# Expert stage of a two-layer diffusion transformer step: 25 tiles of 128 rows, or 14 tiles of four 32-row lists

## What is computed

```python
def moe(h, w_router, router_bias, w_gate_l, w_up_l, w_down_l):
    t = h.reshape(B * N, D)
    scores = jax.nn.sigmoid((t @ w_router).astype(F32))
    sel = scores + router_bias.astype(F32)
    grp = sel.reshape(-1, N_EXPERT_GROUPS, EXPERTS_PER_GROUP)
    best = jnp.argmax(lax.top_k(grp, TOP_K)[0].sum(-1), axis=-1)
    ...
    _, idx = lax.top_k(masked, TOP_K)          # best group, then two experts in it
    w = jnp.take_along_axis(scores, idx, axis=-1)
    w = w / jnp.sum(w, axis=-1, keepdims=True)
    combine = jnp.sum(jax.nn.one_hot(idx, N_EXPERTS, dtype=F32) * w[..., None], axis=1)
    gate = jnp.einsum('td,edf->tef', t, w_gate_l)
    up = jnp.einsum('td,edf->tef', t, w_up_l)
    act = jax.nn.silu(gate) * up * combine[..., None].astype(gate.dtype)
    return jnp.einsum('tef,efd->td', act, w_down_l).reshape(B, N, D)
```

## Time and profile before

| | us |
|---|---|
| median of three runs | 2057.49 |
| lowest and highest run | 2054.66, 2057.91 |
| profiled execution: span, first to last instruction | 2054.5 |
| TensorE busy | 1912.6 (93%) |
| VectorE busy | 1080.4 (53%) |
| ScalarE busy | 884.8 (43%) |
| POOL busy | 314.5 (15%) |
| mean granted TensorE clock | 0.976 of full |
| bytes moved | 336.34 MB, 164 GB/s over the span |

### The profile page before, as it was taken

The page is one execution under the profiler, slowest core; times in us unless marked ns, Lnnn a source line. Parts: engine busy times, 40 slices in busy tenths (PEclk is TensorE's granted clock), DMA queues, the critical chain, the costliest instruction groups (busy, mean ns, idle before and its releaser), DMA issues. The chain is left out here.

```text
span 2054.5 us, 31276 instructions
## 1 busy us (share of the span) xinstructions
PE 1912.6 (93%) x12731; PEld 1617.7 (79%) x12731; DVE 1080.4 (53%) x1766; ACT 884.8 (43%) x1423; POOL 314.5 (15%) x120
## 2 busy tenths in 40 slices
PE   6999999999999979999779998898999998899993
PEld 4899866699999857777578997677999987577762
DVE  4385367641433256777573734665243334577763
ACT  4443455532222235566454435555222233466653
POOL 1303100032224120000111121000212331000003
PEclk9999999999999999999979999999999999999996
DMA  7422477725612159999441220002222222999954
GB/s 262 131 62 64 147 247 256 240 88 199 211 62 73 47 212 361 315 309 318 156 167 44 75 72 13 1 1 92 89 67 72 73 68 114 376 422 369 311 189 174
DMA packets 163921, 336.34 MB, mean 164 GB/s; under 512 B 10434, under 2 KB 121666, under 8 KB 149316
## 3 DMA queue, kind: packets, MB, share of 16 engines
q1 hardware_dynamic: 151488, 299.63, 41.9%
q0 software_dynamic: 5760, 20.97, 2.7%
q10 hardware_dynamic: 6532, 13.74, 2.1%
HBM read 334.58 MB, written 53.74 MB: 189 GB/s over the span
## 5 line engine op out<-in xcount | busy, mean ns | idle before, releaser
L728 POOL TENSOR_TENSOR wlo<-raw,whi 128x2048 fp32r<-128x2048 f32 x46 | 216.1, 4697 | 1053.2 <-ACT whi L752 1053.2
L2007 DVE TENSOR_TENSOR xw_gu_lo<-xw_gu_raw,xw_gu_hi 128x2048 fp32r<-128x2048 f32 x96 | 218.9, 2284 | 53.7 <-ACT xw_gu_hi L1788 35.6
L171 PE MATMUL psum<-h_hi,whi 128*128 128x320 f32 (+2 forms) x896 | 215.3, 313 | 9.0 <-DVE h_lo L156 6.5
L171 PE MATMUL psum<-h_hi,wlo 128*128 128x320 f32 (+2 forms) x896 | 213.0, 310 | 0.0
L171 PE MATMUL psum<-h_lo,whi 128*128 128x320 f32 (+2 forms) x896 | 213.0, 310 | 0.0
L171 PE MATMUL psum<-whi,h_hi 128*128 128x256 f32 x720 | 210.2, 292 | 0.5 <-ACT v_tok L866 0.5
L171 PE MATMUL psum<-wlo,h_hi 128*128 128x256 f32 x720 | 203.6, 283 | 0.0
L171 PE MATMUL psum<-whi,h_lo 128*128 128x256 f32 x720 | 203.6, 283 | 0.0
L1788 ACT ACTIVATE xw_gu_hi<-xw_gu_raw 128x2048 fp32r<-128x2048 f32 x96 | 178.1, 1907 | 7.6 <-DMA xw_gu_raw<-w_e_up 7.6
L2159 PE MATMUL psum<-xw_d_raw,act_T 128*128 128x512 f32 x400 | 179.9, 592 | 0.9 <-ACT act_T L1818 0.9
L832 ACT ACTIVATE prob<-psum,small_stats 128x640 f32<-128x640 f32 (+1 forms) x160 | 112.0, 705 | 133.1 <-DVE small_stats L1194 133.0
(11 more groups left out here) (319 smaller groups left out, 3657.3 us busy)
## 6 DMA issues: line engine op xcount, KB each, us to landing
xw_d_raw<-w_e_down SPq DMA_DIRECT2D x50, 1024.0 KB, 9.0
xw_gu_raw<-w_e_gate SPq DMA_DIRECT2D x48, 1024.0 KB
xw_gu_raw<-w_e_up SPq DMA_DIRECT2D x48, 1024.0 KB
raw<-w_in SPq DMA_DIRECT2D x46, 1024.0 KB, 5.4
wm_rest<-w_mod SPq DMA_DIRECT2D x40, 1024.0 KB, 5.3
y_rows<-y_sel SPq DMA_DIRECT2D x50, 512.0 KB, 9.5
h_sel<-h_rows SPq DMA_DIRECT2D x48, 512.0 KB, 7.5
h_rows<-c_zero ACTq DMA_DIRECT2D x5, 2560.0 KB, 11.2
```

Source lines behind the costliest of these rows:

```text
L171: mm = pe.matmul(dst, st, mv[q], start=start and n == 0, stop=stop and n == 2)
L728: pool.tensor_tensor(wlo[i % 2][:, :, :], raw[i % 2][:, :, :], whi[i % 2][:, :, :].bitcast(F32), ALU.subtract).then_inc(w_lo, 1)
L2007: dve.tensor_tensor(gu_lo[i % 2][:, n, :, :], gu_raw[i % 2][:, n, :, :], gu_hi[i % 2][:, n, :, :].bitcast(F32), ALU.subtract).then_inc(x_l ...
```

## The change

The rows of all experts are laid out in places (slots) of 32 rows, each of one expert: 56 places, in four lists of 14. Tile s has place s of each list, 32 rows of four lists, so that a tile's four quarters can be of four experts. Each list has one copy of its expert's weights on the chip, plain fp32, in three parts: the first half of gate and up by input dimension, the second half, and down. A part is loaded anew only where the list's expert changes; the condition is in a table that VectorE makes. The host lays the weights out in this order (`expert_parts`). The products are whole fp32 products with 32 stationary columns, one after another for the four lists into the four quarters of a bank; nothing is rounded and subtracted. The first tile's rows are read from `h_rows` as the others' are. Loads of rows and most stores of results move from SyncE to ScalarE's queue, a store becomes four of 32 rows, the clearing of `h_rows` covers 14 and not 25 tiles.

```diff
-N_OVER = (2 * TOK - NE) // P
-N_TILES = NE + N_OVER
-SLOTS = N_TILES * P
+N_LISTS, SLOT = 4, 32
+N_SLOTS = (2 * TOK + (SLOT - 1) * NE) // SLOT
+N_TILES = -(-N_SLOTS // N_LISTS)
+N_SLOTS = N_TILES * N_LISTS
...
+        part_at = ((64, 72, 80), (16, 24, 32), (40, 48, 56), (88, 96, 104))
+        xw = [[at(f"xw{q}_{c}", [P, 2048], Z + off * K) for c, off in enumerate(offs)] for q, offs in enumerate(part_at)]
...
                 def _(sp):
+                    w_exp = a["w_expert"][layer].rearrange("e c p n -> c e p n")
...
+                    def list_load(s, q):
+                        v = sp.value_load(slot_i[0:1, q, s:s + 1], min_val=0, max_val=2 * NE - 1)
+                        return v % NE, v < NE
+                    def load_part(c, q, expert, cond):
+                        sp.dma_start(xw[q][c][:, :], w_exp[c][expert, :, :], cond=cond,
+                                     bounds_check="skip_entire_dma").then_inc(xw_ld[c], 16)
...
+                    sp.wait_ge(g_pfree, 24)
+                    for c in range(2):
+                        sp.dma_start(xw[0][c][:, :], w_exp[c][0]).then_inc(xw_ld[c], 16)
+                    sp.wait_ge(o_full, KD)
+                    sp.dma_start(routes[:, :], a["c_route"].partition_broadcast(P)).then_inc(r_c, 16)
+                    sp.dma_start(xw[0][2][:, :], w_exp[2][0]).then_inc(xw_ld[2], 16)
                     low_ready(sp, N_STREAM - 1)
+                    sp.wait_ge(r_st, TAB_STEPS)
+                    firsts = [sp.value_load(slot_i[0:1, q, 0:1], min_val=0, max_val=NE - 1) for q in range(1, N_LISTS)]
+                    for c in range(3):
+                        if c == 2:
+                            sp.wait_ge(k_d, TT)
+                        for q in range(1, N_LISTS):
+                            sp.dma_start(xw[q][c][:, :], w_exp[c][firsts[q - 1], :, :]).then_inc(xw_ld[c], 16)
+                    sp.wait_ge(k_t, KD)
                     sp.wait_ge(k_s, 16 * 2 * TT)
+                    for i in (0, 1):
+                        sp.dma_start(h_sel[i % 2][:, :], h_tiles[i]).then_inc(h_ld[i % 2], 16)
+                    ahead_of = [list_load(1, q) for q in range(N_LISTS)]
                     for i in range(N_TILES):
...
+                            sp.wait_ge(x_h0, i + 1)
+                            for q in range(N_LISTS):
+                                load_part(0, q, *ahead_of[q])
...
+                            sp.wait_ge(x_gu, i + 1)
+                            for q in range(N_LISTS):
+                                load_part(1, q, *ahead_of[q])
...
+                        if i >= 1:
+                            sp.wait_ge(x_dn, 2 * i)
+                            for q in range(N_LISTS):
+                                load_part(2, q, *now[q])
...
                 def _(act):
...
+                    def store_y(i, lists):
+                        act.wait_ge(x_y0, i + 1)
+                        act.wait_ge(x_y1, i + 1)
+                        for q in lists:
+                            act.dma_start(y_tiles[i][q], y_sel[i % 2][list_rows(q), :]).then_inc(y_st[i % 2], 16)
...
+                    for i in range(N_TILES):
+                        if i >= 1:
+                            keep_act(i - 1)
+                        if 1 <= i < N_TILES - 1:
+                            keep_h(i + 1)
+                        if i >= 2:
+                            keep_y(i - 2)
+                            store_y(i - 2, range(N_LISTS))
+                        if i < N_TILES - 2:
+                            load_h(i + 2)
+                        sigmoid(i)
...
                 def _(dve):
...
+                    step(dve.tensor_tensor(slot_ends[:, :, :], over_1[:, 0:NE - 1].unsqueeze(1).to_broadcast([P, N_SLOTS, NE - 1]),
+                                           ends_at, ALU.is_le))
+                    step(dve.tensor_reduce(slot_e[:, :, 1:N_TILES + 1], slot_ends[:, :, :].rearrange("p (q s) e -> p q s e", q=N_LISTS),
+                                           AX.X, ALU.add))
+                    step(dve.tensor_tensor(slot_same[:, :, :], slot_e[:, :, 1:N_TILES + 1], slot_e[:, :, 0:N_TILES], ALU.is_equal))
...
                 def _(pe):
...
                     def gate_up(i):
+                        pe.wait_ge(x_hk, i + 1)
                         if i >= 2:
                             pe.wait_ge(x_ac, i - 1)
                         for kc in range(KD):
-                            pe.matmul(dst, hT_hi[i % 2][:, kc, :], gu_hi[i % 2][:, :, kc, :], start=(kc == 0), stop=False)
-                            pe.matmul(dst, hT_lo[i % 2][:, kc, :], gu_hi[i % 2][:, :, kc, :], start=False, stop=False)
+                            c, k = divmod(kc, KD // 2)
+                            if k == 0:
+                                pe.wait_ge(xw_ld[c], 16 * N_LISTS * (i + 1))
+                            for q in range(N_LISTS):
+                                mm = pe.matmul(psum[list_rows(q), i % 2, :], hT[i % 2][:, kc, q, :], xw[q][c][:, k * 512:(k + 1) * 512],
+                                               start=(kc == 0), stop=(kc == KD - 1))
+                            if kc == KD // 2 - 1:
+                                mm.then_inc(x_h0, 1)
                         mm.then_inc(x_gu, 1)
...
+                    turn_h(0)
+                    for i in range(N_TILES):
+                        if i >= 1:
+                            turn_act(i - 1)
+                        if i >= 1 and i + 1 < N_TILES:
+                            turn_h(i + 1)
                         gate_up(i)
+                        if i == 0:
+                            turn_h(1)
+                        else:
+                            down(i - 1)
...
+def expert_parts(gate, up, down):
+    gate_up = np.stack([w.reshape(DEPTH, NE, P, KD, DE) for w in (gate, up)], axis=4)
+    halves = gate_up.reshape(DEPTH, NE, P, 2, KD * DE).transpose(0, 1, 3, 2, 4)
+    return np.ascontiguousarray(np.concatenate([halves, down.reshape(DEPTH, NE, 1, P, 2 * D)], axis=2))
```

More of the change, by code:

```diff
@@ L578, in build, with list_rows @@
         x_step = sem("moe_residual")
-        tiles = []
-        for e in range(NE):
-            tiles.append(("s", e))
-            if e % 2 == 1:
-                tiles.append(("o", e // 2))
-        tiles += [("o", j) for j in range(NE // 2, N_OVER)]
-        assert len(tiles) == N_TILES
-        def row0(i):
-            kind, n = tiles[i]
-            return (n if kind == "s" else NE + n) * P
+        h_tiles = h_rows.rearrange("(q s r) d -> s r q d", q=N_LISTS, s=N_TILES)
+        y_tiles = y_rows.rearrange("(q s r) d -> s q r d", q=N_LISTS, s=N_TILES)
+        def list_rows(q):
+            return slice(q * SLOT, (q + 1) * SLOT)
         LOGIT_STEPS = 4
         ROUTE_STEPS = 15
-        ROW_STEPS = 28
-        IDX_STEPS = 44
+        TAB_STEPS = 26
+        ROW_STEPS = 33
         for layer in range(DEPTH):
@@ L2285 @@
     arrays = {n: np.ascontiguousarray(inputs[n]) for n in INS}
+    arrays["w_expert"] = expert_parts(inputs["w_e_gate"], inputs["w_e_up"], inputs["w_e_down"])
     arrays.update(constants())
```

303 lines of the change are left out of this document (84 added, 219 removed).

## The result

| | before | after |
|---|---|---|
| median of 4 runs | 2057.7 us (2054.66 to 2058.12) | 2044.2 us (2039.84 to 2048.63) |
| ratio | | 0.994, 95% interval 0.9923 to 0.9956 |
| profiled execution, span | 2054.5 us | 2041.0 us |
| first layer, first gate-and-up to last down product | 756.8 to 1016.2: 259.4 us | 790.26 to 1003.10: 212.8 us |
| second layer | 1749.6 to 2009.5: 259.9 us | 1771.44 to 1993.03: 221.6 us |

The change makes the kernel faster, by 13.5 us. I had forecast 67.5 us, so four fifths of the gain are missing. The page of the changed kernel, in the order of the earlier trace rows: three lines of the 40 slices, the queues (packets, MB, share), the memory line, and the chain by engine.

The account below looks back on a forecast made before the run. TensorE was taken to bound the kernel. First layer 30.4 + 169.5 + 18 + 4.5 + 5 - 259.4 = -32.0 us, second -35.5, together -67.5 from 2057.5: 1990 us, range 1930 to 2055.

Parts of the forecast that it names:

- The bound and the new tile: Expert stage: TensorE sets the pace; a new tile costs it 12.15 us, a layer of 14 takes 169.5 us against 259.
- Rival C: Expert-stage products: four quarters overlap less well over a whole stage than in a short burst; 2043 us, chance 0.08.
- The start: Start of a layer's expert stage: the first layer's first product comes at 787.2 us, 30.4 us later than before.
- the burst: Before the first product: nine weight loads, scattered rows and the row load, 15.2 MB at 0.42 MB/us, 36.2 us.
- The loads inside the stage: Reloads of the single weight copies between tiles: waits of 18 us in the first layer, 15 us in the second.
- the clock: TensorE's clock falls again after pauses for loads within the stage: 5 us a layer, bounds 0 and 10.
- The ledger: Step-by-step walk through a layer's 13 tile changes, one queue at 0.42 MB/us also carrying 1.05 MB of rows a tile.
- the twos: Steps between tiles where two lists change expert: a wait of 0.6 to 1 us at a lone one.
- this case's own range: Whole kernel: 1950 to 2035 us around the forecast of 1990 us, without the rivals.
- Rival B: Single weight copy and first burst: queues become the bound, at 315 GB/s; 217 us for the tiles, 2078 us, chance 0.11.
- Rivals A and D: Expert-stage weight loads: A, they disappear, 1925 us, chance 0.15; D, they aren't skipped, 2460 us, chance 0.02.
- The other edits: Clearing of h_rows, last stores through two queues, later loads of the next layer's weights: all taken at nothing.

Follow-up runs that it names:

- s7: The changed kernel with first weight loads of parts 1 and 2 of lists 1 to 3 moved behind the first row loads: 2035.42 us.
- s1_static: The changed kernel with only the wanted weight loads, the places of expert changes written into the program: 2038.02 us, ratio 0.9925 to the kernel before.
- s9: s1_static with the 15 expert changes a layer spread evenly over the steps, loads without condition: 2007.07 us.
- s10: s1_static with row loads and row stores on ScalarE's queue moving a quarter of their columns from the third tile on: 2000.57 us.
- s16: s1_static with weight loads a tile earlier into buffers no product reads, and row loads a tile earlier into a third buffer: 1958.74 us.
- s3: The changed kernel with no weight load in the expert stage after the first tiles', neither wanted nor skipped: 1949.42 us.
- s14: The changed kernel with first part 1 and 2 loads of lists 1 to 3 later, row loads ahead of ScalarE's copy and stores: 2040.82 us.

## Why the prediction was right or wrong

**The bound and the new tile: right.** The earlier trace rows carried over to whole products: 7.08 us for 64 (7.0 forecast), 3.62 for 32 (3.6), and 11.7 us for a tile that waits for nothing (12.15). Without weight loads a layer's stage is 168.8 and 170.4 us, which holds the half-clock first product and the uncovered last activation; I had 169.5 and 4.5 for those, 174. Rival C is out. The Trainium skill ("TensorE: Matmul & The Clock Gate", Part 3) has 2.38 times for three column tiles, 79% of three; four here gave 64 x 0.43 / 7.08 = 3.9 times, 97% of four, and the trace doesn't agree with that share.

**The start: near, 3 to 5 us short.** The table of experts was there at 743.4 (743.5 forecast), the scatter began at 747.3 (747.4), and the first product at 790.26, 33.5 us later than before instead of 30.4. I had put the row load's bytes into the burst; in fact it is issued when the scatter has landed, at 783.27, and lands 3.9 us behind it. That the burst of 9 loads is what delays the scatter is shown by s7: issue at 766.9.

**The loads inside the stage: the step that failed.** I forecast 18 and 15 us of waits and 5 for the clock. Waits on loads were 38.6 and 36.9 us. Against the stage without loads, the changed kernel's is 44.0 and 51.2 us longer; 35.5 and 37.1 of that are more waits of any kind (39.3 and 40.6 less 3.8 and 3.5), most of the rest products and transposes at the half clock behind them (5.81 us for the last down product above, 3.62 otherwise; the granted clock was 0.59 from 990 to 1010). In the first layer the last step, where three lists change, cost 20.4 us (6.45 + 2.32 + 11.60) where I had 15.7 (2.8 + 4.0 + 8.9). The ledger broke at the twos: they and the steps behind them waited 18.2 us in the first layer, where I had some 2 to 3, and 21.5 in the second, where I had some 6.

First, the rows were no waiter in my ledger, only bytes: a row load is issued 4.2 us into a tile, behind four stores, and was late at nine places in two layers (827.38 above is one), 6.9 and 8.3 us. Second, what is asked for in a step with two lists takes longer to carry than I had it. A load that is alone was priced rightly: the first two of s1_static's stage land 4.8 us after issue, and I had 4.9. The 45 of the stage take 7.6 in the median, and the fourth of the first step with two lists, issued 3.95 us behind the first of them, takes 11.2; the product waited 1.98 and 1.93 us for these four, where I had 0.6 to 1 in all:

```profile
xw<-w_expert SPq DMA_DIRECT2D x2, 1024.0 KB, 4.8
```

```profile
xw<-w_expert SPq DMA_DIRECT2D x45, 1024.0 KB, 7.6
```

```profile
xw<-w_expert SPq DMA_DIRECT2D x1, 1024.0 KB, 11.2
```

It is not that the engines were slow then. Windows of the changed kernel that are nothing but waits of TensorE on loads (PE busy, granted clock, DMA share, GB/s):

```profile
824.70:827.38 2.68, 0.00 (x1) 1.00 0.99 408
963.79:970.24 6.45, 0.00 (x1) 0.79 1.01 389
1810.11:1813.67 3.56, 0.01 (x1) 0.58 1.02 426
1819.19:1823.80 4.61, 0.00 (x1) 1.00 1.02 427
```

So the 0.42 MB/us held in the waits, or nearly (over the 11.60 us ahead of the last down product it was 343 GB/s). Everything that a step wants is asked for within a few us, rows and weights together, and TensorE waits while the engines carry it at full rate; in between the engines have less to do, because no buffer is free, and the mean is 306 GB/s. The experiments put sizes to it: the spread over the steps (s9, 14 and 13 us), the bytes of the rows (s10, 10 us) and lead for weights and rows (s16, 40 and 35 of 44 and 45 us). They don't add up, since they share the same engines. Which term of my walk through the twos was short, apart from the rows', stays open: with a quarter of the row bytes (s10) a tile with two lists still took 15.0 to 16.2 us.

The measured 2044 us lies within the stated 1930 to 2055, but outside this case's own range of 1950 to 2035. The wider one reached that far for the sake of rival C, which didn't happen; that it holds the result is luck.

**Rival B: half right.** It named the place (a part is only issued after a product) and was given 0.11. Its rate over a stretch was measured too, 306 GB/s over 800 to 960 in the changed kernel, and its 217 us for the tiles is the mean of 212.8 and 221.6. But that rate is no limit of the engines: in s16 they carried up to 421. Treated as a limit, it also slowed the first burst, which in fact ran at full rate (416 GB/s from 750 to 780), and so gave 2078, too slow; that it met the tiles' time is in part luck. The Trainium skill ("DMA: Bandwidth & Descriptors", Bandwidth) has 425 GB/s for a transfer of 16 MB issued from GpSimd, and the traces agree with it for loads that queue, with 421 in s16 and up to 427 in the waits above. The limit of 358 GB/s for one core in the Trainium skill ("DMA: Bandwidth & Descriptors", Specifications), from which I had worked out 2033 us, doesn't agree with the 421. Rivals A and D are out: loads were late, and skipped ones moved nothing.

**The other edits.** The end was 2.9 us longer than before, where I had nothing: from the last down product to the first gather it took 4.9 us in the second layer (1993.03 to 1997.90), 3.7 before (2009.46 to 2013.13), and the rest came behind the gather. In the first layer it took 4.8 us (1003.10 to 1007.93), 4.0 before.

**The account.** Start 3.1 in the first layer and 4.6 at the second (with what the first layer's end lost), stages 212.8 + 221.6 where I had 197 + 194, 43.4; end 2.9: 54.0 us, the difference between 67.5 and 13.5.

## What to carry to other kernels

A single copy of a buffer is safe only where its reload, with all that the neighbours ask for at the same moment, fits into the window between last and next use; count every transfer as a waiter too, not only as bytes. Look at the worst steps, not at the mean: 62 MB in 212 us looks like slack, and four steps of thirteen decide. A low GB/s in a long window is demand until a run with more lead has shown otherwise, and a look at the GB/s within the waits says it sooner.

## What the runs showed that I had not expected

- The memory line of the page counts loads that a condition skips: 514.08 MB with every load of the stage skipped, in 1950.77 us, against 186.93 MB without them, in 1949.42 us. A branch in SyncE's program in place of the condition came out 5 to 7 us slower, at the edge of the noise.
- Four products on quarters of the array ran 3.9 at a time for a whole stage; a tile took 11.7 us whether the DMA engines had little to do (84 GB/s in s3) or carried 421 GB/s (s16).
- An early load can cost more than a late one: earlier row loads, worth 22.9 us in the first layer when the weights had lead (195.1 to 172.2, a third buffer), lost 9 (ratios) to 12 us (medians) in s14, where they had none.
- Not tried: a kernel with two copies of all weights and the right output. The four lists' parts take 96 KB of each partition, and the loads are conditional, so that which copy is the current one is only known when the kernel runs.
